# Gates and memory queries of layer one by seven half products; head norms, states and memory attention placed by slots; three row blocks begun with five rows of weights

## The chip, the cores and the metric

One core of one Trainium2 chip runs the kernel. The metric is device microseconds (us) of one launch, the median of several runs. Five engines work side by side: TensorE (PE: matmuls, all in float32 here, and transposes), VectorE (DVE), ScalarE (ACT), GpSimd (POOL) and SyncE (SP), which here only issues DMAs. They are ordered by semaphores alone, which the program sets by hand.

## The reference

One step of a decoder of two layers, on 1024 prompt rows and 8 sample rows (W = 1032 columns once they are laid side by side), model width 1024. The change touches layer one, cut here to what matters:

```python
h = _rmsnorm(x, g_pre);  z = h @ w_in_a                      # 1024 -> 4096
u, o_pre, zg, qm, zm = split(z, [1024, 2048, 3072, 3584])
# u gives q, k, v; a scan over 8 chunks of 128 gives hs for 4 heads of 256
C_new = dc * C + einsum('s,sv,sk->vk', ws, v, k)              # also for 8 x 4 sample states
h = sigmoid(o_pre) * hs
hn = (h - mean(h)) * rsqrt(var(h) + EPS) * g_hn               # per head
ya = (hn + skip * xc) * silu(zg)
ym = mem_attention(qm, mk, mv) * silu(zm)                     # 256 memory rows, 4 heads of 128
x = x + _rmsnorm(concat([ya, ym]) @ w_out_a, g_post)
```

Layer two (windowed attention and memory attention) then follows in the same manner. The 32 sample states C (8 samples, 4 heads, 256x256) are read, decayed, updated and written back.

## The kernel before

Activations lie transposed: HT holds h as eight tiles of 128 features by 1032 columns, BIG holds 24 such tiles, a head h of layer one having six of them from 6h on. RING is three slots of weights, PS eight PSUM banks. The stages, in the order in which TensorE meets them:

- Stages 0 and 1: memory keys and values, the norm, the projections u, q, k, v, the gate rows, and the first o projection pair (o0). They stay as they are.
- Stage 2 (`stage2_pe` and its like on each engine): 32 units, 8 chunks by 4 heads. In a unit TensorE makes scores (L744), transposes v and k (L750, L752), transposes the finished rows of two units ago (L762), then the numerator (L772, L775) and the state update (L783). L762 waits for `ct_done`, which DVE gives by its two updates of L866. On DVE a unit is L837 (q scaled, both inputs in SBUF), L841 (scores by decay), three tiny operations (L852 to L859), L866 twice. POOL only adds the mask to each chunk's rows (L728). Behind the loop the states of the prompt are transposed (L882).
- Stage 3 (`stage3_pe`, `stage3_act`, `stage3_dve`, `stage3_pool`, `stage3_sp`): the projections zg0, then o, zg of the heads 1 to 3, each by `pe_proj` (L301): 8 weight tiles times 3 segments of 344 columns, 24 matmuls. Between them come the averages of a head over its features (L1071, `average`), which wait for DVE's sums. DVE works in the order of the heads: for each, eight sample states (`pair_dve`: L1031 a reduce, L1036 two updates), the gate o as one operation of 2064 columns (L1204), the sum of both tiles (L1206), and between the next head's states the centring (L1170), the sum of squares (L1163), the norm (L1150, L1153) and the gate zg (L1158). ACT applies sigmoid and silu while it reads a projection out of PSUM (L1130, L1137), takes the squares (L1097), makes the root by Ln and Exp (L1105, L1107) and decays states (L1024). POOL multiplies a state by q (L1017). SP loads and stores states in three buffers of XTRA.
- Stage 4: the queries qmA and the gates zmA of the memory attention by the same kind of projection (L301, L1819), 4 tiles each. While zmA runs, the 18 steps of `step_pe` (scores L1670, transposes L1682, values L1702) are woven between its matmuls; their softmax lies on DVE (L1741 to L1759) and ACT (L1723). The silu of zmA comes when all of it is done (L1636).
- Stage 5 (`out_pe`): the output projection by blocks of 128 rows, each 12 weight rows `kt` (8 of the heads, 4 of the memory attention) by two halves of 512 columns (L1970); the last rows by columns (L2014). Block 0 and block 1 run their 8 head rows first, block 2 comes whole after both. The samples' attention is woven in (L1453, L1469, L1514).
- Layer two (`layer_b_*`): its projections go by pairs of output tiles, `PAIRS`. The half-size blocks of weights and activations are combined so that seven products do the work of eight (`ORDER`: A11 B11, S2 T2, A12 B21, S3 T3, S1 T1, A22 T4, S4 B22). A pair has two units (column halves, `BOUNDS` 0-256-512 and 512-772-1032), a unit seven products of four matmuls (L2844), a product is a **slot**, 14 slots a pair. POOL makes the weight sums (`sum_pair`, L2460 to L2464), DVE the four activation sums T (`h_sum`, L2401), once per layer. Of a unit's products ACT copies two out of PSUM (j = 0 and 2, L2929), DVE adds the other five (`product_sum_dve`, L3023 to L3034), and all else in layer two is placed by the number of the slot.

`product_waits` is what binds TensorE to these:

```python
elif j == 2: pe.wait_ge(*copied(u, 0))      # ACT's copy of product 0
elif j == 3: pe.wait_ge(*summed(u, U2))     # DVE's sum of product 1
elif j == 6: pe.wait_ge(*summed(u, C22))    # DVE's sum of product 4
```

So the sums of the products 1 and 4 must be done one slot after their product ended; those of 3, 5 and 6 have two slots or more.

## Time and profile before

| | us |
|---|---|
| median of 3 runs (lowest, highest) | 1902.46 (1899.45, 1902.49) |
| the profiled execution, its own time | 1904.15 |
| its span in the trace | 1902.4 |
| PE busy in the span | 1858.9 (98%) |
| DVE / ACT / POOL busy | 772.0 / 591.8 / 361.2 |
| PE's share of the chain that ended last | 89% |
| data moved | 196.14 MB |

The profile lists each float32 matmul as two records, so its counts are twice those of the code. The end of a matmul record is modelled and reaches past the start of the next: how fast TensorE streams is read from the length of an unbroken run of records, divided by their number, not from the mean duration of one. A group of instructions is named by the line of the kernel that issued it.

### The profile page before, as it was taken

The numbers are of one execution on the slowest core, as the hardware profiler recorded it, in microseconds if no ns is written. First come the engines' busy times: TensorE is split into PE (matmuls) and PEld (weight loads), VectorE is DVE, ScalarE is ACT, GpSimd is POOL, SyncE is SP. The second block draws the span as 40 slices with busy tenths as digits, with TensorE's granted clock in tenths as the row PEclk, the third lists the DMA queues.
The fourth block names the chain that finished last, engine by engine and source line by source line (L and its number), as shares of the span: only waits on it lengthen the run. The fifth ranks groups of instructions, "written<-read, shape, count | busy, mean of one in ns | idle before, by whom it ended". The sixth has DMA issues, their size and how long they took to land.

```text
span 1902.4 us, 21176 instructions
## 1 busy us (share of the span) xinstructions
PE 1858.9 (98%) x8117; PEld 1368.1 (72%) x8117; DVE 772.0 (41%) x1470; ACT 591.8 (31%) x1362; POOL 361.2 (19%) x309
## 2 busy tenths in 40 slices
PE   7999999999999999999999999999999999999998
PEld 3566664678666666765756888888888888878673
DVE  0332210555253542445144254335434544676523
ACT  1512231555243322341131122432233234643311
POOL 0000000010131110122002344225422643122100
PEclk9999999999999999999999999999999999999999
DMA  7311210211555652464110111123223342845322
GB/s 270 108 66 61 68 45 11 69 37 45 132 189 166 210 166 80 87 197 135 45 68 32 45 45 57 62 73 100 79 68 99 92 155 90 269 134 159 130 89 90
DMA packets 163215, 196.14 MB, mean 103 GB/s; under 512 B 19275, under 2 KB 122315, under 8 KB 162978
## 3 DMA queue, kind: packets, MB, share of 16 engines
q1 hardware_dynamic: 132628, 163.49, 27.6%
q10 hardware_dynamic: 30486, 31.30, 5.3%
q8 instruction: 65, 1.06, 0.2%
q14 instruction: 36, 0.29, 0.1%
HBM read 156.97 MB, written 37.85 MB: 102 GB/s over the span
## 4 chain that ended last, share of the span: by engine, by line
PE 89%; DVE 3%; ACT 3%; issue 2%; DMA 1%; POOL 1%; SPq 0%; ACTq 0%; DVEq 0%; POOLq 0%
PE PS L2844 29%; PE PS L301 17%; PE PS L1970 10%; PE PS L502 4%; PE PS L2014 4%; PE PS L1670 3%; PE PS L1819 3%; PE PS L381 3%; PE PS L512 2%; PE PS L1705 2%; PE PS L1682 2%; PE PS L1702 1%; PE PS L783 1%; PE PS L775 1%; DVE WK L866 1%
## 5 line engine op out<-in xcount | busy, mean ns | idle before, releaser
L301 PE MATMUL PS<-HT,RING 128*128 128x344 f32 x1344 | 391.2, 453 | 1.6 <-DVE HT L459 1.2
L301 PEld LDWEIGHTS PS<-HT,RING 128*128 128x128 f32 x1344 | 254.9, 190 | 135.9 <-DVE HT L459 2.0
L2844 PE MATMUL PS<-HT,RING 128*128 128x260 f32 (+1 forms) x1152 | 293.3, 383 | 1.2 <-ACT BIG L2929 1.2
L2844 PEld LDWEIGHTS PS<-HT,RING 128*128 128x128 f32 x1152 | 213.1, 191 | 29.4 <-ACT BIG L2929 1.9
L1970 PE MATMUL PS<-BIG 128*128 128x512 f32 x352 | 156.9, 596 | 0.0
L1723 ACT ACTIVATE WK<-PS,WK 128x256 f32<-128x256 f32 (+1 forms) x160 | 68.9, 435 | 189.6 <-DVE WK L1741 186.3
L2929 ACT ACTIVATE BIG<-PS 128x256 f32<-128x256 f32 (+1 forms) x96 | 37.0, 386 | 258.5 <-PE PS L2844 258.4
L1970 PEld LDWEIGHTS PS<-BIG 128*128 128x128 f32 x352 | 64.9, 190 | 72.4 <-issue 72.2
L1741 DVE TENSOR_REDUCE WK<-PS 128x2 f32<-128x512 f32 (+1 forms) x80 | 48.3, 604 | 108.0 <-PE PS L1670 107.8
L728 POOL TENSOR_TENSOR WK<-WK,CST 128x512 f32<-128x512 f32 x8 | 10.2, 1281 | 424.4 <-DMA WK<-mlstm_rows 424.4
L2844 PE MATMUL PS<-HT,CST 128*128 128x256 f32 (+1 forms) x336 | 86.4, 382 | 0.1
L1017 POOL TENSOR_TENSOR WK<-XTRA 128x512 f32<-128x512 f32 x32 | 48.6, 1522 | 199.8 <-DMA XTRA<-sample_q_and_weighted_k 161.5
L502 PE MATMUL PS<-WK,RING 128*128 128x344 f32 x288 | 83.9, 452 | 0.0
L2438 ACT ACTIVATE RING<-RING,VEC 128x256 f32<-128x256 f32 x176 | 75.0, 502 | 1.7 <-DMA RING<-in_w_in_b 0.8
L502 PEld LDWEIGHTS PS<-WK,RING 128*128 128x128 f32 x288 | 54.7, 190 | 28.7
L2844 PE MATMUL PS<-WK,RING 128*128 128x256 f32 x288 | 73.8, 380 | 0.0
L2844 PE MATMUL PS<-BIG,RING 128*128 128x260 f32 x288 | 71.4, 384 | 0.2 <-DVE BIG L3023 0.2
L3043 DVE TENSOR_TENSOR BIG<-BIG,TRIG 64x1024 f32<-64x1024 f32 (+1 forms) x48 | 71.2, 1482 | 1.1
L2844 PEld LDWEIGHTS PS<-HT,CST 128*128 128x128 f32 x336 | 61.7, 190 | 8.6 <-DVE BIG L3028 0.8
L2713 POOL TENSOR_TENSOR BIG<-BIG 128x512 f32<-128x512 f32 x48 | 61.0, 1282 | 13.4 <-DVE BIG L3052 13.4
L381 PE MATMUL PS<-RING,BIG 128*128 128x512 f32 x128 | 59.0, 622 | 3.2 <-ACT BIG L413 2.0
L1819 PE MATMUL PS<-HT,RING 128*128 128x344 f32 x192 | 61.8, 453 | 0.0
(350 smaller groups left out, 2930.4 us busy)
## 6 DMA issues: line engine op xcount, KB each, us to landing
WK<-in_cache_mem_kv SPq DMA_DIRECT2D x56, 256.0 KB, 5.8
RING<-in_w_kv_b SPq DMA_DIRECT2D x12, 1024.0 KB, 5.3
RING<-in_w_in_b SPq DMA_DIRECT2D x12, 1024.0 KB, 5.3
RING<-in_w_in_a ACTq DMA_DIRECT2D x21, 512.0 KB, 4.2
WK<-in_cache_win SPq DMA_DIRECT2D x40, 256.0 KB, 5.0
RING<-in_w_mkv SPq DMA_DIRECT2D x16, 512.0 KB, 4.7
BIG<-in_x_prompt SPq DMA_DIRECT2D x16, 512.0 KB, 3.2
XTRA<-in_state_C SPq DMA_DIRECT2D x32, 256.0 KB, 3.4
```

The source lines that it names most:

```text
L301: last = nc.tensor.matmul(PS[:, s + b, 0:SEG], w[:, kt * P:(kt + 1) * P], rhs(kt, b * SEG, (b + 1) * SEG), start=(kt == 0), stop=(kt == kt ...
L381: last = nc.tensor.matmul(PS[:, 4 * l + 2 * nt + half, :], MEMT[:, kt, nt * P:(nt + 1) * P], w[:, half * 512:(half + 1) * 512], start=(kt ...
L502: last = nc.tensor.matmul(PS[:, s + b, 0:SEG], w[:, c:c + P], rhs, start=(kt == 0), stop=(kt == 1))
L1670: last = nc.tensor.matmul(bank[:, x * nk:(x + 1) * nk], q, k, start=(g in MEM), stop=True, skip_group_check=True)
L1723: last = nc.scalar.activation(PROB[:, u % 2, x * nk:(x + 1) * nk], PS[:, 3 + u % 2, x * nk:(x + 1) * nk], ACT.Exp, bias=negmax[:, x:x + 1] ...
L1819: last = nc.tensor.matmul(PS[:, b, 0:SEG], w[:, kt * P:(kt + 1) * P], ht(kt, b * SEG, (b + 1) * SEG), start=(kt == 0), stop=(kt == KT - 1))
L1970: last = nc.tensor.matmul(PS[:, BANKS[i] + half, :], c.src(kt, u * P, (u + 1) * P), c.piece(kt)[:, half * 512:(half + 1) * 512], start=(kt ...
L2014: last = nc.tensor.matmul(PS[:, 6 + n % 2, 0:COLS], c.piece(kt)[:, n * P:(n + 1) * P], c.src(kt, 6 * P, W), start=(kt == 0), stop=(kt == c ...
L2438: last = nc.scalar.activation(x, x, ACT.Copy, scale=VEC[:, k, row:row + 1])
L2713: last = nc.gpsimd.tensor_tensor(perm(dst, d)[:, j0:j1], natural(big(RAW + x, 0, T), d)[:, j0:j1], natural(big(TURN + x, 0, T), d)[:, j0:j ...
L2844: last = nc.tensor.matmul(PS[:, bank, 0:mid - lo], weight_block(u // 2, s, k), h_block(u % 2, t, k), start=(k == 0 and j not in (2, 3, 6)) ...
L3043: last = nc.vector.tensor_tensor(y[q:q + 64], x[p:p + 64], TRIG[p:p + 64, W + lo:W + hi] .rearrange("p (t n) -> p t n", t=1).to_broadcast( ...
```

## The change

In layer one, 22 projection tiles (zg0 to zg3, o1 to o3, the memory queries and their gates) now go by the seven products too, as 11 pairs in the order zg0, o1, zg1, o2, zg2, o3, qm01, qm23, zg3, zm01, zm23, with bounds 0-258-516 and 516-774-1032: 154 slots. Of TensorE's matmuls nothing else changes in kind or number: 528 of 344 columns become 616 of 258. The stages 3 and 4 become one table of slots, `layer_a_*`:

```diff
-        for h in range(H):
-            if h > 0:
-                oz_jobs(h, D, "o")
...
+        for x, first in (("Azg0", 2 * D), ("Ao1", D + 2 * P), ("Azg1", 2 * D + 2 * P), ("Ao2", D + 4 * P),
+                         ("Azg2", 2 * D + 4 * P), ("Ao3", D + 6 * P), ("Aqm01", 3 * D), ("Aqm23", 3 * D + 2 * P),
+                         ("Azg3", 2 * D + 6 * P), ("Azm01", 3 * D + 4 * P), ("Azm23", 3 * D + 6 * P)):
+            PAIRS.append((x, w_in_a, first, None))
+        PA = len(PAIRS)
...
+        EARLY_AT = (17, 18, 19, 23, 25, 27, 29, 31)
...
+        XA = 14 * PA
+        GATE, GATED_3 = (4, 31, 58, 86), 128
+        MEAN = [x + 3 for x in GATE]
+        VAR = [x + 9 for x in GATE]
+        KEYS_A, STEPS_A = 112, 116
...
+        def states_at(x):
+            return [i for i in range(EARLY_STATES, H * NS) if 3 + 7 * (i - EARLY_STATES) // 2 == x]
...
+        def layer_a_dve(dve):
+            for x in range(XA + 1):
+                if x >= 1:
+                    product_sum_dve(dve, x - 1)
+                for i in states_at(x - 1):
+                    pair_dve(dve, i)
+                for h in range(H):
+                    head_dve(dve, x, h)
+                for s in steps_a(x):
+                    step_dve(dve, MEM_A, s)
+                for n in keys_a_at(x - 1):
+                    samples_scores_dve(dve, "A", [n])
```

`head_dve` cuts a head's work into operations of one tile (1032 columns) at fixed slots behind `GATE[h]`: n = 0, 1 the gate o (n = 0 also the sample part), 2 the sum for the mean, 4, 5 the centring, 8 the sum of squares, 12, 13 and 14, 15 the norm, 16, 17 the gate zg (head 3: slots 128, 129). The averages stand inside the slots `MEAN` and `VAR` on TensorE and wait there for DVE. Sigmoid and silu are now applied by ACT in place, on two tiles of half the columns, one slot after a unit is complete (`gate_act`), so the silus of zg3 and zm fall among the steps of the memory attention, which begin at slot 116 and come every second slot.

Eight of the 32 sample states move into stage 2, behind the units of `EARLY_AT`, on POOL, ACT, DVE and SP; the other 24 come every three or four slots, with a fourth buffer. POOL, not DVE, makes layer one's sums of activations:

```diff
+            if c == 2:
+                pool.wait_ge(job_done.sem, done("o0_1"))
+                for gi in range(2):
+                    h_sum(pool, "A", gi, T1)
+                sum_pair(pool, 0)
...
+            pool.wait_ge(sig("kv_turned").sem, NU - 2)
+            h_sum(pool, "A", 0, T2), h_sum(pool, "A", 0, T3)
+            pair_pool(pool, EARLY_STATES - 1)
```

In stage 5 five weight rows come first, in each of the blocks 0, 1 and 2, and then the other seven of each; the samples' values move behind with them:

```diff
-                self.kts, self.early, self.src, self.piece = kts, kts - H, src, piece
+                self.kts, self.early, self.src, self.piece = kts, 5 if kts > KT else 4, src, piece
...
-            block_products(pe, x, 0, early[:4])
+            block_products(pe, x, 0, early)
             free1(pe)
             samples_pe(pe, x)
-            block_products(pe, x, 0, early[4:])
...
+            block_products(pe, x, 1, early)
+            samples_turned_pe(pe, x)
+            if x == "A":
+                block_products(pe, x, 2, early)
```

The weight rows 2 and 3 are loaded once the last unit but one is done, the rows 5 to 7 once the last product is.

On TensorE, from the end of stage 2 on, before (L301 a projection of 24, L1071 an average):

```order
L783 MATMUL PS<-WK 128x257 x2
L882 MATMUL PS<-CST,WK 128x128 x8
L762 MATMUL PS<-CST,WK 128x128 x2
L882 MATMUL PS<-CST,WK 128x128 x8
L301 MATMUL PS<-HT,RING 128x344 x96
L1071 MATMUL PS<-BIG,CST 128x344 x3
```

and now (L2952 is a product's matmul, L896 the old L882, L1198 the old L1071):

```order
L793 MATMUL PS<-WK 128x257 x2
L896 MATMUL PS<-CST,WK 128x128 x8
L772 MATMUL PS<-CST,WK 128x128 x2
L2952 MATMUL PS<-HT,RING 128x258 x4
L2952 MATMUL PS<-BIG,WK 128x258
L896 MATMUL PS<-CST,WK 128x128 x8
L2952 MATMUL PS<-BIG,WK 128x258 x3
L2952 MATMUL PS<-HT,RING 128x258 x4
L2952 MATMUL PS<-BIG,RING 128x258 x4
L2952 MATMUL PS<-HT,RING 128x258 x4
L2952 MATMUL PS<-BIG,RING 128x258 x4
L2952 MATMUL PS<-HT,CST 128x258 x4
```

The average that had four whole projections ahead of it now has seven products and one matmul.

On DVE, the gate of head 1 (behind 16 states) with the states around it, before:

```order
L1031 TENSOR_REDUCE SM<-WK 128x2
L1036 SCALAR_TENSOR_TENSOR XTRA<-XTRA,SM 128x256 x2
L1196 TENSOR_TENSOR SM<-SM 128x16
L1197 TENSOR_TENSOR SM<-SM 128x16
L1199 TENSOR_TENSOR BIG<-SM 128x2x8
L1204 TENSOR_TENSOR BIG<-BIG 128x2064
L1206 TENSOR_TENSOR BIG<-BIG 128x1032
L1031 TENSOR_REDUCE SM<-WK 128x2
```

and now (L1070 and L1075 are a state, L1335 the gate o of one tile, L1338 the sum, L31xx sums of products):

```order
L1317 TENSOR_TENSOR SM<-SM 128x16
L1318 TENSOR_TENSOR SM<-SM 128x16
L1320 TENSOR_TENSOR BIG<-SM 128x2x8
L1335 TENSOR_TENSOR BIG<-BIG 128x1032
L3137 TENSOR_TENSOR BIG<-BIG,PS 128x258
L1070 TENSOR_REDUCE SM<-WK 128x2
L1075 SCALAR_TENSOR_TENSOR XTRA<-XTRA,SM 128x256 x2
L1335 TENSOR_TENSOR BIG<-BIG 128x1032
L3140 TENSOR_TENSOR BIG<-BIG,PS 128x258
L1338 TENSOR_TENSOR BIG<-BIG 128x1032
L3143 TENSOR_TENSOR BIG<-BIG,PS 128x258
L3146 TENSOR_TENSOR BIG<-BIG,PS 128x258
```

The sums that TensorE waits for within a slot now stand in DVE's queue behind whole-tile operations and states.

## Rows read from the trace of the kernel before

**Rows 1.** The page's first part: busy time, share of the span, instructions.

```profile
PE 1858.9 (98%) x8117; PEld 1368.1 (72%) x8117; DVE 772.0 (41%) x1470; ACT 591.8 (31%) x1362; POOL 361.2 (19%) x309
```

**Rows 2.** Stretches (us: length, PE PEld DVE ACT POOL busy, PEclk, DMA, GB/s).

```profile
360.80:480.80 120.00, 111.63 (x648) 94.47 (x649) 66.48 (x243) 67.04 (x167) 11.05 (x9) 1.00 0.15 42
480.80:840.50 359.70, 356.18 (x1373) 243.21 (x1371) 154.13 (x242) 111.13 (x179) 66.71 (x47) 1.00 0.52 147
840.50:1024.00 183.50, 183.50 (x638) 106.96 (x637) 64.87 (x104) 39.28 (x91) 13.97 (x9) 1.00 0.28 98
1042.80:1132.20 89.40, 89.40 (x412) 78.09 (x413) 31.46 (x49) 16.81 (x43) 30.98 (x30) 1.00 0.15 47
```

**Rows 3.** The chain that ended last, in order of time: start, length, what.

```profile
556.00 41.64 PE PS L301 x144
...
840.64 6.87 PE PS L1970 x16
...
1281.86 38.25 PE PS L2844 x176
```

**Rows 4.** Groups of TensorE between 480.8 and 840.4 us.

```profile
L301 PE MATMUL PS<-HT,RING 128*128 128x344 f32 x864 | 251.3, 452 | 0.0
L1819 PE MATMUL PS<-HT,RING 128*128 128x344 f32 x192 | 61.8, 453 | 0.0
```

**Rows 5.** Waits of TensorE between 480 and 841 us: total, times, longest.

```profile
PE PS L1071 <- DVE BIG L1163: 1.8, 1, 1.8
```

**Rows 6.** DVE in stage 2, in order of time, and POOL's operation there.

```profile
425.21 1.45 DVE L837 TENSOR_TENSOR WK<-BIG,WK 128x256 f32<-128x256 f32 x1
...
430.18 0.29 DVE L841 TENSOR_TENSOR WK<-PS,WK 128x128 f32<-128x128 f32 x1 [0.97 <-ACT WK L811]
430.71 0.16 DVE L852 SCALAR_TENSOR_TENSOR SM<-PS,SM 128x1 f32<-128x1 f32 x1 [0.24 <-PE PS L775]
...
431.57 0.88 DVE L866 SCALAR_TENSOR_TENSOR WK<-WK,PS 128x257 f32<-128x257 f32 x2 [0.32 <-PE PS L783]
...
425.11 1.27 POOL L728 TENSOR_TENSOR WK<-WK,CST 128x512 f32<-128x512 f32 x1 [12.32 <-DMA WK<-mlstm_rows]
```

**Rows 7.** By source line: shortest, median, longest (ns), first and last start.

```profile
L837 DVE TENSOR_TENSOR WK<-BIG,WK x32: 415/418/1497, 359.1 to 471.7; 128x256 f32<-128x256 f32 x32
L1031 DVE TENSOR_REDUCE SM<-WK x32: 674/682/690, 480.4 to 691.2; 128x2 f32<-128x512 f32 x32
L1036 DVE SCALAR_TENSOR_TENSOR XTRA<-XTRA,SM x64: 469/479/1484, 487.3 to 692.2; 128x256 f32<-128x256 f32 x64
L1163 DVE TENSOR_TENSOR BIG<-BIG x4: 1233/1434/2053, 552.6 to 707.9; 128x1032 f32<-128x1032 f32 x4
L3023 DVE TENSOR_TENSOR BIG<-BIG,PS x48: 410/422/427, 1028.8 to 1755.0; 128x256 f32<-128x256 f32 x24, 128x260 f32<-128x260 f32 x24
L1105 ACT ACT_TABLE_LOAD  x4: 1283/1283/1283, 555.0 to 718.4; - x4
L1137 ACT ACTIVATE BIG<-PS x8: 1010/1031/1034, 494.9 to 687.9; 128x1032 f32<-128x1032 f32 x8
```

**Rows 8.** Groups by engine and shape (busy us, mean ns, idle before).

```profile
L1036 DVE SCALAR_TENSOR_TENSOR XTRA<-XTRA,SM 128x256 f32<-128x256 f32 x64 | 30.8, 523 | 60.8 <-ACT XTRA L1024 60.3
L1163 DVE TENSOR_TENSOR BIG<-BIG 128x1032 f32<-128x1032 f32 x4 | 6.2, 1538 | 8.0 <-ACT BIG L1097 8.0
L2462 POOL TENSOR_TENSOR WK<-RING 128x512 f32<-128x512 f32 x12 | 19.2, 1603 | 0.9
L1017 POOL TENSOR_TENSOR WK<-XTRA 128x512 f32<-128x512 f32 x32 | 48.6, 1522 | 199.8 <-DMA XTRA<-sample_q_and_weighted_k 161.5 <-PE PS L783 35.9 <-DVE SM L1031 2.3
```

**Rows 9.** DMA issues: KB each, median us from issue to landing.

```profile
RING<-in_w_in_b SPq DMA_DIRECT2D x12, 1024.0 KB, 5.3
XTRA<-in_w_out_a ACTq DMA_DIRECT2D x3, 512.0 KB, 8.8
```

More of the change, by code:

```diff
@@ new lines, in gate_applied, with tiles2, keys_a_at, steps_a @@
+        def gate_applied(kind, n):
+            u = 2 * [x[0] for x in PAIRS].index(kind) + n
+            return sig("tables_applied").sem, sum(1 for k in range(u + 1) if gated(k))
+        TABLES_A = sum(1 for k in range(2 * PA) if gated(k))
+        def tiles2(t, lo=0, hi=W):
+            return BIG[:, :].rearrange("p (i w) -> p i w", w=W)[:, t[0]:t[1] + 1:t[1] - t[0], lo:hi]
+        def keys_a_at(x):
+            return [n for n in range(2 * NS) if 122 + 2 * n == x]
+        def steps_a(x):
+            return [s for s in range(18) if STEPS_A + 2 * s == x]
@@ new lines, in layer_a_pool @@
+        def layer_a_pool(pool):
+            for x in range(XA):
+                for i in states_at(x + 1):
+                    pair_pool(pool, i)
+                if x == 6:
+                    pool.wait_ge(sig("h_turned").sem, NU)
+                    sum_pair(pool, 1)
+                p = x // 14 + 1
+                if x % 14 == 9 and 2 <= p < PA:
+                    sum_pair(pool, p)
+                samples_pool(pool, "A", keys_a_at(x))
+            samples_pool(pool, "A", [n for n in range(2 * NS) if 122 + 2 * n >= XA])
@@ L1066, in average @@
+        AVERAGED = PS[:, 3:6, 0:SEG]
         def average(pe, name, h, summed):
-            pe.wait_ge(*slot_free(name))
             pe.wait_ge(sig(summed).sem, h + 1)
+            if name == "mean0":
+                pe.wait_ge(sig("c_copied").sem, H)
+            else:
+                pe.wait_ge(*read_of(f"mean{h}" if name[0] == "v" else f"var{h - 1}"))
             for b in range(3):
-                last = nc.tensor.matmul(PS[:, slot_of(name) + b, 0:SEG], avg_h,
-                                        big(h * 6 + 2, b * SEG, (b + 1) * SEG), start=True, stop=True)
+                last = nc.tensor.matmul(AVERAGED[:, b, :], avg_h, big(HELD[h][0], b * SEG, (b + 1) * SEG),
+                                        start=True, stop=True)
@@ new lines, in woven_a_pe, with layer_a_pe, first_copy_act @@
+            if x == KEYS_A + 2:
+                memory_query_pe(pe, 0)
+                yield
+            for s in steps_a(x):
+                yield from step_pe(pe, MEM_A, s)
+        def layer_a_pe(pe):
+            for x in range(XA):
+                woven = woven_a_pe(pe, x)
+                product_pe(pe, x, woven)
+                for _ in woven:
+                    pass
+        def first_copy_act(act, u):
+            kind = PAIRS[u // 2][0]
+            if kind == "Ao2":
+                act.wait_ge(sig("conv_saved").sem, 32 + 16 * H)
+            if kind == "Azg2":
+                act.wait_ge(sig("y_ready").sem, 2)
+            if kind == "Ao3":
+                act.wait_ge(sig("squares_summed").sem, 2)
+                act.wait_ge(job_done.sem, done("var0"))
+            if kind == "Aqm01":
+                act.wait_ge(job_done.sem, done("var1"))
+            if kind == "Aqm23":
+                act.wait_ge(sig("y_ready").sem, 4)
+                act.wait_ge(job_done.sem, done("var2"))
+            if kind == "Azg3":
+                act.wait_ge(sig("y_ready").sem, 6)
+            if kind == "Azm01":
+                act.wait_ge(job_done.sem, done("var3"))
+            if kind == "Azm23":
+                act.wait_ge(sig("squares_summed").sem, 3)
@@ L2077, in both @@
                 hold(kt)
-            block_products(pe, x, 2, range(c.kts), both)
-            column_products(pe, x, 0, early)
+            block_products(pe, x, 2, range(c.kts) if x == "B" else late, both)
+            column_products(pe, x, 0, own)
             pe.wait_ge(sig("sample_out_read").sem, order + 1)
-            column_products(pe, x, 0, late)
+            column_products(pe, x, 0, cross)
             for n in range(1, KT):
```

767 lines of the change are left out of this document (385 added, 382 removed).

## The prediction

> **What bounds the kernel now.** I read the page's busy times first: TensorE (PE) is busy for 1858.9 of 1902.4 us, DVE for 772.0 [rows 1]. Busy time can hide small gaps, because the ends of matmuls are modelled, so I took two more views. The stretches show where PE has room: from the end of stage 2 to the start of the output projection it lacks 3.5 us of 359.7, in the output projection nothing of 183.5, in stage 2 8.4 of 120.0 [rows 2]. The chain of waits gives the pace of an unbroken run: 144 records of 344 columns in 41.64 us, 0.2892 us each, and 176 records of layer two's products, 256 and 260 columns in equal parts, in 38.25 us, 0.2173 us each [rows 3]. Both are near 0.84 ns per column. The kernel streams columns from end to end, at the full clock (granted 1.00 in these stretches [rows 2], the 2.4 GHz level). So a column less is worth 0.84 ns twice over, and nothing else brings anything unless it removes one of the few waits. A change that gives other engines more to do costs time only where PE comes to wait.
>
> **Columns.** Between 480.8 and 840.4 us lie 864 + 192 = 1056 records of 344 columns [rows 4]: 22 tiles of 24 matmuls, two records each. At 0.2892 us they take 305.4 us. The 154 products have 616 matmuls, 1232 records of 258 columns, the mean width of the run in layer two: 1232 x 0.2173 = 267.7 us. **-37.7 us**. The weights of a matmul change every 258 columns now and not every 344; the same run in layer two shows no cost of that, its 0.2173 us holds it. All other matmuls keep their number and width in the order of the instructions, so that the change does what it says on PE can be taken as settled.
>
> **Waits that go.** The 3.5 us of idle PE in that stretch [rows 2] are mostly one average waiting 1.8 us for DVE [rows 5], and the places where the others lie are laid out anew. **-3 us**; I price the new ones apart.
>
> **Stage 2.** 32 units fill 120 us, some 3.6 us each [rows 2]. DVE is idle in it for 0.97 + 0.24 + 0.32 = 1.53 us, and its L866 stands on PE's path: PE goes on with L762 when it is done [rows 6]. A state adds 0.68 + 2 x 0.48 = 1.64 us to DVE [rows 7], 0.1 us more than that room, and some 0.1 us for its semaphores; ACT's decay and POOL's product have room or lie on another engine. Eight states, the last of them behind the last unit: 1.5 us. Then POOL. In rows 6 DVE's L837, two operands from SBUF, takes 1.45 us and not 0.42, beside a POOL operation of 1.27 us that began 0.10 us earlier; the longest L837 took 1.50 [rows 7], while L3023, one of whose operands is PSUM, never passes 0.43 [rows 7]. Its delay of 1.03 us disappeared in the 1.53. The activation sums on POOL have 1032 columns: 1.27 x 1032 / 512 = 2.6 us if it goes by length, so they can delay L837 by up to 2.5 us, 1.0 beyond the room. Of the eight, two fall at the start and three before the last unit: 4.5 us with the states' updates caught too. **+6 us**, ends 1.5 (no operation is caught) and 12 (each early state is also caught once by 0.75 us). The early activation sums and the first weight sums themselves are hidden: the first product with a sum that comes late, S3 T3, begins 3.5 us after stage 2, and POOL's row of T2, T3, a state and T4 begins two units, 7 us, before its end. Without that cover a late sum would cost 2.6 us each.
>
> **DVE in the slots.** A slot is 8 x 0.2173 = 1.74 us. DVE's sum of a product takes 0.42 [rows 7]; products 1 and 4 of a unit leave it one slot. A head's whole-tile operations take 1.23 us at the least [rows 7]. At two places per head the queue is too full.
> - Gate and mean. Three slots and one matmul, 3 x 1.74 + 0.43 = 5.65 us, are there before PE wants the head's sum for its average. DVE has in them three tiles (3.7), a state (1.64), the sample part (0.5) and three product sums (1.26) for head 0: 7.1 us, 1.45 late; two product sums for the heads 1 and 2: 6.7, 1.05 late each; head 3 has no state there and is in time. 3.5 us.
> - Norm and gate zg. Six slots, 10.4 us, and about one slot of grace, for six tiles (7.6), two states (3.3) and four product sums (1.7), 12.6 us: 0.5 us for each of the heads 0 to 2, 1.5 us.
>
> That is 5 us with no operation lengthened. Operations with two operands in SBUF were lengthened on average from 0.48 to 0.52 (states) and from 1.23 to 1.54 (the sum of squares) [rows 7, 8], with POOL busy for 66.7 of 359.7 us [rows 2]. Now POOL has besides 24 states of 1.5 us [rows 8] ten weight sums of four operations near 1.5 and a short one, close to 7 us a pair of 24.3 us: half of the time up to slot 92. I take 0.15 us per operation, between 0.04 and 0.31: 15 of them in the first places, 2.3 us, and 30 in the second, of which half falls into the grace, 2.2 us. **+9.5 us**, ends 5 and 15 (0.3 us each).
>
> The page "SBUF — State Buffer" of the Trainium skill, in "Who interferes with whom", says that a DVE instruction with two SBUF inputs and a GpSimd instruction that reads SBUF exclude each other for the whole instruction, whoever comes first. By that rule alone, with POOL busy half of the time and half an operation left on average, the hold would be near 0.3 us, this term 15 and the whole sum 5.5 us higher. The trace agrees in kind: 1.45 against 0.42 [rows 6].
>
> **ACT beside the memory attention.** Silu among the Exps of the steps costs ACT two table loads of 1.28 and 1.03 us of work [rows 7], 3.6 us in a step of 2 x 1.74 us and 2.2 us of attention matmuls; between a step's scores and its transposes lie some 6 us of PE work against a chain of 3.3 us on DVE and ACT. It happens at slots 120, 127, 134, 141. **+1 us**, ends 0 and 6.
>
> **Output projection.** The same products, in another order, and PE had no gap in it [rows 2], so there is nothing to gain. Five rows of three blocks are 30 matmuls of 2 x 0.43 us [rows 3], 25.8 us before anything else is needed, against 27.5 before (two blocks of eight rows). The rows 2 and 3 are issued seven slots (12.2 us) before block 0, and 1 MB lands in 5.3 us, with ACT's rows beside it in up to 8.8 [rows 9]. **0**, ends 0 and 3.
>
> **Sum.** -37.7 - 3 + 6 + 9.5 + 1 = -24.2 us, on the profiled execution's 1904.15 us (its span is 1902.4) 1880.0. The profiled execution lies 1.7 above the median of the runs shown; for a median, 1902.46 - 24.2 = **1878 us**. With all low ends it is -34, with all high ends -5.
>
> **Rivals.**
> - Nobody waits. In layer two PE ran 89.4 us without a gap with DVE 35% and POOL 35% busy [rows 2]. If the queue's lateness is taken up by the slack of two slots, only 1.5 us of stage 2 remain: -39, 1863 us. Against it: layer one's DVE has 129 us of work in the first 92 slots (160 us), 80%.
> - DVE becomes the bound, and the kernel slower. Mechanism: POOL's operations hold DVE's two-operand ones. There are 48 state updates and 40 head operations up to slot 92. At 0.8 us each, near the longest holds seen (1.48 - 0.48, 2.05 - 1.23 [rows 7]), DVE's 129 us become 199 against 160: +39; stage 2 at 12, less 40.7: +10, 1913 us. It decides from about 0.7 us per operation. Against it: the mean holds of 0.04 and 0.31. The page named above makes it possible but does not give the holds.
> - States are late. The 32 states went from 487.3 to 692.2 us, 6.5 us each [rows 7], and POOL waited 161.5 us for their loads [rows 8]. Now one is due every 3.5 slots, 6.1 us, with a weight pair of 1 MB every 24.3 us in the same queue. If they come no faster, DVE stands still with product sums behind it: 24 x 0.5 = 12 us more, 1890 us. Against it: a fourth buffer, loads issued some 9 slots ahead, and DMA at 0.52 [rows 2], with ACT's pace, not the loads, behind half of the waits before.
>
> **How the numbers follow.** Forecast 66% (its own range 1868 to 1889), nobody waits 14%, states late 10%, DVE the bound 6%, other mishaps that end near or above the old time 4%. 0.2% is 3.8 us, about what a measurement of this kernel tells from no change. Faster by more: 91%; within: 2%; slower: 7%. The range for 8 in 10 is 1862 to 1893: it takes in the case without waits and late states, and leaves the bound DVE and the tail of the high ends out.
>
> **What would show it.** Right: no record of 344 columns but u, o0, qkv, gates and averages, runs of products at 0.217 us each, some 318 us from the last L793 to the first block plus 10 of waits; PE's waits led by products and averages (L1198) waiting for DVE near slots 6, 7, 20, 34, 40, 61 and 76; stage 2 longer by 4 to 8 us, with DVE's scaling of q at 2 us beside POOL's sums; output projection of 183 us as before. Wrong: PE idle by less than 5 us in the slots (first rival), POOL or DVE waiting for state loads (third), DVE busy above 90% up to slot 92 with updates near 1.3 us (second), or a gap at the first block, waiting for weights.

## The result and the profile after

In 15 runs each, the changed kernel took 1908.08 us in the median (1897.25 to 1916.08) and the kernel before 1900.7 us (1898.35 to 1903.93). The ratio is 1.0035, 95% interval 1.0023 to 1.0047: slower by 0.35%, where 1.3% faster was forecast, and outside the range. The profiled run took 1906.62 us, its span is 1904.8. The runs of the change spread over 19 us, those of the kernel before over 5.6; their mean granted clock lies between 0.987 (the run of 1916.08 us) and 0.995 (the run of 1897.25).

The busy times of the page answer to [rows 1]:

```profile
PE 1834.1 (96%) x8293; PEld 1405.8 (74%) x8293; DVE 838.9 (44%) x1588; ACT 606.1 (32%) x1397; POOL 446.8 (23%) x372
```

PE has 24.8 us less to do and the span is 2.4 us longer. The stretches answer to [rows 2], with the same columns (start:end, length, busy of PE, PEld, DVE, ACT, POOL, granted clock, DMA share, GB/s): stage 2, the slots of layer one, the output projection.

```profile
358.10:488.80 130.70, 114.63 (x640) 96.66 (x641) 87.39 (x264) 69.74 (x170) 43.04 (x29) 0.96 0.26 80
488.80:843.00 354.20, 331.50 (x1556) 280.73 (x1554) 198.54 (x342) 126.69 (x212) 122.09 (x93) 0.98 0.45 135
843.00:1026.50 183.50, 183.50 (x636) 107.04 (x637) 68.54 (x101) 35.54 (x87) 13.01 (x7) 1.00 0.26 95
```

From stage 2's first transposes to the first product it is now 130.8 us and was 119.7; from there to the output projection 354.2 and was 359.7. The output projection is unchanged, as forecast. Stage 2 began 3.1 us earlier, in code that the change doesn't touch: in the loading phase the trace of the kernel before has three stretches of 3.4 us at the half clock, that of the change one. So 2.4 = -3.1 + 11.1 - 5.5 - 0.1. The forecast had +6 for stage 2 and -30.2 for the slots. The other new thing is the granted clock: 0.96 and 0.98 where it was 1.00 twice. The waits of TensorE from 358 to 843 us, total, times and longest:

```profile
PE PS L772 <- DVE WK L878: 9.2, 3, 5.0
PE PS L2952 <- DVE BIG L3140: 6.4, 4, 2.2
PE PS L1198 <- DVE BIG L1338: 5.1, 3, 3.0
PE PS L2952 <- ACT BIG L3040: 4.7, 1, 4.7
PE PS L1198 <- DVE BIG L1348: 3.3, 3, 1.9
PE PS L2952 <- DVE BIG L3135: 2.5, 3, 1.0
```

L2952 is a product, L1198 an average, L772 a unit's turned values in stage 2. Three causes can be read from the trace.

**Stage 2's end.** DVE, then POOL, in order of time:

```profile
463.38 4.69 DVE L1075 SCALAR_TENSOR_TENSOR XTRA<-XTRA,SM 128x256 f32<-128x256 f32 x2
467.99 0.41 DVE L849 TENSOR_TENSOR WK<-BIG,WK 128x256 f32<-128x256 f32 x1
...
475.44 3.35 DVE L1075 SCALAR_TENSOR_TENSOR XTRA<-XTRA,SM 128x256 f32<-128x256 f32 x2
478.72 2.41 DVE L849 TENSOR_TENSOR WK<-BIG,WK 128x256 f32<-128x256 f32 x1
```

```profile
463.07 2.39 POOL L2502 TENSOR_TENSOR BIG<-HT 128x1032 f32<-128x1032 f32 x1
465.53 2.25 POOL L2502 TENSOR_TENSOR BIG<-BIG,HT 128x1032 f32<-128x1032 f32 x1
...
473.80 2.21 POOL L2502 TENSOR_TENSOR BIG<-BIG,HT 128x1032 f32<-128x1032 f32 x1
475.96 2.55 POOL L2502 TENSOR_TENSOR BIG<-HT 128x1032 f32<-128x1032 f32 x1
478.66 4.54 POOL L2502 TENSOR_TENSOR BIG<-BIG,HT 128x1032 f32<-128x1032 f32 x2
```

At 463 us both updates of a state (L1075) are held, each until the activation sum then running ends: together they take 4.69 us instead of 0.88. At 475 us the second update is held in the same way (3.35 us for the two), and q's scaling (L849) meets the next sum and takes 2.41 us. The sums come back to back, so an operation of DVE with two operands in SBUF that has stood out one of them can meet the next, and the delays add up: PE waits 3.5 us from 466.4 and 5.0 us from 477.6. With both waits TensorE's clock falls.

**Slot 14.** ACT, in order of time, POOL's product of a state, and the products of PE on both sides:

```profile
524.16 0.72 ACT L1061 ACTIVATE TRIG<-TRIG,SM 128x512 f32<-128x512 f32 x1 [6.98 <-POOL WK L1052]
524.90 1.28 ACT L1262 ACT_TABLE_LOAD   x1
526.19 1.12 ACT L1262 ACTIVATE WK<-PS,SM 128x1032 f32<-128x1032 f32 x1
527.33 1.28 ACT L1264 ACT_TABLE_LOAD   x1
528.63 1.06 ACT L1264 ACTIVATE WK<-WK 128x1032 f32<-128x1032 f32 x1
529.60 0.37 ACT L3040 ACTIVATE BIG<-PS 128x258 f32<-128x258 f32 x1
```

```profile
522.86 1.27 POOL L1052 TENSOR_TENSOR WK<-TRIG 128x512 f32<-128x512 f32 x1 [8.25 <-DMA TRIG<-sample_q_and_weighted_k]
```

```profile
523.38 1.91 PE L2952 MATMUL PS<-BIG,WK 128*128 128x258 f32 x8
530.02 3.81 PE L2952 MATMUL PS<-HT,RING 128*128 128x258 f32 x8 [4.73 <-ACT BIG L3040]
```

The copy of product 14 (L3040) stands behind head 0's root (Ln and Exp, each with a table load, 4.7 us), the root behind the decay of a state, and the decay waits 6.98 us for POOL's product, which waits 8.25 us for its load. The load was late in SP's queue, behind this wait for the small stores of stage 2's states and four loads of xc:

```profile
SPq L1138 <- DMA out_m_p<-SM: 12.9, 1, 12.9
```

**The clock.** Eight records (four matmuls) of 258 columns took 1.91 us before that wait and 3.81 us behind it. Six stretches at the level of 1.2 GHz lie in stage 2 and the slots, beginning at 470.8, 481.0, 528.8, 542.5, 627.8 and 661.9 us, and none in the kernel before. Three of them, with the columns as above, and the sum of the six:

```profile
470.80:474.20 3.40, 3.40 (x10) 2.74 (x9) 0.91 (x5) 1.18 (x3) 1.63 (x2) 0.50 0.24 85
...
528.80:535.60 6.80, 5.58 (x13) 4.45 (x14) 2.83 (x3) 5.12 (x7) 1.30 (x1) 0.50 0.70 238
542.50:545.90 3.40, 3.40 (x10) 2.65 (x9) 3.40 (x3) 0.00 (x0) 3.24 (x3) 0.50 0.18 45
...
sum 27.40, PE 24.46 PEld 18.96 DVE 11.66 ACT 8.24 POOL 16.23; mean PE 4.08 PEld 3.16 DVE 1.94 ACT 1.37 POOL 2.70
```

Each lies in or right behind a pause of PE of 2 us or more. In them PE is busy for 24.5 us, half of which is loss: some 12 us.

### The profile page after: what moved, and what is told of

It is laid out like the page before. It is cut to its first block, busy times and chain, and to the rows that moved or that the text cites. A ratio compares the mean times of both kernels' runs of the same rounds, so it can differ in the third digit from the quotient of the medians.

```text
span 1904.8 us, 21851 instructions
## 1 busy us (share of the span) xinstructions
PE 1834.1 (96%) x8293; PEld 1405.8 (74%) x8293; DVE 838.9 (44%) x1588; ACT 606.1 (32%) x1397; POOL 446.8 (23%) x372
## 4 chain that ended last, share of the span: by engine, by line
PE 87%; DVE 5%; ACT 3%; issue 3%; DMA 1%; POOL 1%; ACTq 0%; DVEq 0%; SPq 0%; POOLq 0%
PE PS L2952 40%; PE PS L2055 10%; PE PS L282 7%; PE PS L483 4%; PE PS L2099 4%; PE PS L1856 3%; PE PS L362 2%; PE PS L493 2%; PE PS L1891 2%; PE PS L1868 2%; PE PS L1888 1%; PE PS L793 1%; PE PS L785 1%; DVE WK L878 1%; PE PS L1694 1%
## 5 line engine op out<-in xcount | busy, mean ns | idle before, releaser
L2952 PE MATMUL PS<-HT,RING 128*128 128x260 f32 (+2 forms) x1680 | 425.1, 384 | 5.9 <-ACT BIG L3040 5.9
L2952 PEld LDWEIGHTS PS<-HT,RING 128*128 128x128 f32 x1680 | 313.6, 192 | 49.6 <-ACT BIG L3040 7.0
L3040 ACT ACTIVATE BIG<-PS 128x256 f32<-128x256 f32 (+2 forms) x140 | 54.0, 385 | 405.9 <-PE PS L2952 405.5
L282 PE MATMUL PS<-HT,RING 128*128 128x344 f32 x480 | 139.9, 453 | 1.6 <-DVE HT L440 1.2
L2952 PE MATMUL PS<-BIG,RING 128*128 128x260 f32 (+1 forms) x560 | 138.7, 383 | 1.1 <-DVE BIG L3135 1.0
L282 PEld LDWEIGHTS PS<-HT,RING 128*128 128x128 f32 x480 | 90.9, 190 | 50.3 <-DVE HT L440 2.0
L2952 PEld LDWEIGHTS PS<-BIG,RING 128*128 128x128 f32 x560 | 105.1, 191 | 17.5 <-DVE BIG L3135 1.9
L2952 PE MATMUL PS<-BIG,WK 128*128 128x258 f32 (+1 forms) x448 | 112.7, 385 | 1.5 <-DVE BIG L3135 1.5
L2952 PE MATMUL PS<-HT,CST 128*128 128x256 f32 (+2 forms) x432 | 110.8, 383 | 1.3 <-DVE BIG L3140 1.2
L2952 PEld LDWEIGHTS PS<-BIG,WK 128*128 128x128 f32 x448 | 84.4, 193 | 14.4 <-DVE BIG L3135 2.5
L2952 PEld LDWEIGHTS PS<-HT,CST 128*128 128x128 f32 x432 | 79.4, 190 | 13.6 <-DVE BIG L3140 3.2
L2952 PE MATMUL PS<-WK,RING 128*128 128x256 f32 x288 | 73.8, 380 | 0.0
L3137 DVE TENSOR_TENSOR BIG<-BIG,PS 128x256 f32<-128x256 f32 (+1 forms) x70 | 29.5, 422 | 97.7 <-PE PS L2952 97.4
```

The source lines that it names most:

```text
L282: last = nc.tensor.matmul(PS[:, s + b, 0:SEG], w[:, kt * P:(kt + 1) * P], rhs(kt, b * SEG, (b + 1) * SEG), start=(kt == 0), stop=(kt == kt ...
L2952: last = nc.tensor.matmul(PS[:, bank, 0:mid - lo], weight_block(u // 2, s, k), h_block(layer_of(u), u % 2, t, k), start=(k == 0 and j not ...
L3040: nc.scalar.activation(big(n2 if j == 0 else n1, lo, mid), PS[:, banks(u)[0], 0:mid - lo], ACT.Copy).then_inc(sig("projections_copied").up ...
```

## The experiments

All are edits of the changed kernel. Each was timed in five rounds against the kernel before on its chip (the probe and the last one in three). "Against the change" is the ratio's difference from 1.0035, times 1901 us; two such ratios have together an uncertainty of 3 to 4 us, near 5 for the probe and the last run. The last two columns are from each trace: from stage 2's first transposes to the first product, and from there to the output projection (the kernel before: 119.7 and 359.7).

| run | ratio to before (95%) | against the change | stage 2 | slots |
|---|---|---|---|---|
| the change | 1.0035 (1.0023 to 1.0047) | | 130.8 | 354.2 |
| e1, late activation sums narrow | 0.9972 (0.9960 to 0.9984) | -12.0 | 119.4 | 352.0 |
| e2, root behind the copy | 1.0012 (0.9996 to 1.0029) | -4.4 | 132.3 | 350.0 |
| e3, POOL's slot work narrow | 0.9960 (0.9949 to 0.9972) | -14.3 | 132.2 | 339.0 |
| e4, slot states narrow | 0.9948 (0.9936 to 0.9960) | -16.5 | 131.7 | 336.3 |
| e5, xc's loads at slot 10 | 0.9996 (0.9982 to 1.0009) | -7.4 | 131.6 | 342.9 |
| e6, sums shared with DVE | 0.9971 (0.9958 to 0.9985) | -12.2 | 119.7 | 351.8 |
| e7, e5 and e6 | 0.9952 (0.9938 to 0.9966) | -15.8 | 119.7 | 345.5 |
| e8, six pauses in layer two | 1.0118 (1.0099 to 1.0136) | +15.8 | 132.7 | 352.5 |
| e9, e7 and a state first | 0.9950 (0.9936 to 0.9965) | -16.2 | 119.6 | 344.6 |
| e10, e9 and averages later | 0.9943 (0.9930 to 0.9956) | -17.5 | 119.4 | 346.4 |
| e11, averages later alone | 1.0000 (0.9989 to 1.0011) | -6.7 | 132.8 | 345.9 |
| e12, all light | 0.9847 (0.9825 to 0.9868) | -35.7 | 119.9 | 330.5 |

### e1: the late activation sums narrow

```diff
+            if layer == "A" and (gi, t) != (0, T1) and (gi, t) != (1, T1):
+                out, x, y = out[:, :, 0:8], x[:, :, 0:8], y[:, :, 0:8]
             on.tensor_tensor(out, x, y, ALU.subtract).then_inc(sig("h_sums").up(), 1)
```

> The changed kernel with the six activation sums that GpSimd makes at the end of stage 2 cut from 258 columns a block to 8, so that part of the activations' sums is left out; all waits stay. Theory of the holds: the long gaps at 466.1 (3.64 us) and 477.2 (5.18 us) come from DVE's updates of two SBUF operands being held for some 2 us each by these sums of 2.3 to 2.6 us, and the 10 us at the half clock behind them follow from the gaps: stage 2 falls from 130.7 to 120 to 123 us and the kernel by 8 to 11 us. Theory of the full queue: the eight states' updates alone fill DVE in stage 2: the kernel falls by 3 us at the most and stage 2 stays above 127.

Measured: -12.0 us, stage 2 at 119.4 with a granted clock of 1.00. The whole 11 us of stage 2 come from six operations on an engine off the critical path. That is the theory of the holds; the full queue's would have left stage 2 above 127 us. The eight early states cost nothing: with them stage 2 is as long as before.

### e2: head 0's root behind the copy

```diff
-                    if x == VAR[h] + 1:
+                    if x == VAR[h] + (2 if h == 0 else 1):
                         root(act, h)
```

> The changed kernel with ACT's logarithm and exponential of head 0's variance one slot later, behind the copy of product 14 and no longer ahead of it. If that order makes the gap of 4.89 us at 524.9 and, through it, the 6.8 us at the half clock behind it (3.4 us lost), the kernel falls by 5 to 8 us. Rival: the norms on DVE and all behind them are then late instead, and the gap only moves to a product that waits for DVE: less than 2 us.

Measured: -4.4 us, between the two expectations. The wait for the copy fell from 4.7 to 0.3 us, but the root, now at 529.3 to 534.0 us, made the norms late, and a product sum behind them: one wait of 5.5 us, for L3140 at slot 20. The order of root and copy is a link of the chain, not its start.

### e3: POOL's work in the slots narrow

The ten weight sums (from the second pair on) and the 24 state products of the slots are cut to 8 columns; DVE reads another tile of the same width for the state's sum.

```diff
-                QWP(i, 0, 256).unsqueeze(1).to_broadcast([P, 2, 256]), ALU.mult)
+                QWP(i, 0, m).unsqueeze(1).to_broadcast([P, 2, m]), ALU.mult)
...
+            if 1 <= p < PA:
+                cut = lambda t: t[:, :, 0:8]
+                a11, a21, a22, s2, s3 = cut(a11), cut(a21), cut(a22), cut(s2), cut(s3)
```

> The changed kernel with GpSimd's part of the slots of layer one taken down to 8 columns an operation (the ten weight sums from the second pair on and the 24 state products, so that these parts of the computation are left out); DVE and ACT keep all their instructions and widths. Theory of the holds: DVE's operations of 2 us there return to 0.42 and 1.23 us, PE's idle 23 us in the slots falls below 12, and fewer half-clock stretches follow: the kernel falls by 12 to 18 us. Theory of the full queue: DVE has too much at the places of the heads whatever GpSimd does: 6 us at the most, and the waits for the sums of the heads stay.

Measured: -14.3 us, the slots 15.2 us shorter, with DVE's instructions and widths all there. The groups of DVE between 488 and 843 us show why: busy time and mean ns of one, first in the change, then here (each line number is one higher):

```profile
L1075 DVE SCALAR_TENSOR_TENSOR XTRA<-XTRA,SM 128x256 f32<-128x256 f32 x38 | 27.4, 763 | 0.7 <-ACT XTRA L1061 0.7
L1368 DVE TENSOR_TENSOR BIG<-BIG 128x1032 f32<-128x1032 f32 x8 | 13.8, 1726 | 0.6 <-ACT BIG L1269 0.6
L1360 DVE SCALAR_TENSOR_TENSOR BIG<-WK,VEC,BIG 128x1032 f32<-128x1032 f32 x8 | 12.9, 1629 | 0.1
L1343 DVE TENSOR_TENSOR BIG<-BIG,PS 128x1032 f32<-128x1032 f32 x8 | 9.7, 1219 | 0.0
L1338 DVE TENSOR_TENSOR BIG<-BIG 128x1032 f32<-128x1032 f32 x4 | 8.1, 2026 | 0.0
```

```profile
L1076 DVE SCALAR_TENSOR_TENSOR XTRA<-XTRA,SM 128x256 f32<-128x256 f32 x38 | 16.6, 479 | 0.6 <-ACT XTRA L1062 0.5
L1361 DVE SCALAR_TENSOR_TENSOR BIG<-WK,VEC,BIG 128x1032 f32<-128x1032 f32 x8 | 10.1, 1286 | 0.1
L1369 DVE TENSOR_TENSOR BIG<-BIG 128x1032 f32<-128x1032 f32 x8 | 10.0, 1245 | 0.6 <-ACT BIG L1270 0.6
L1344 DVE TENSOR_TENSOR BIG<-BIG,PS 128x1032 f32<-128x1032 f32 x8 | 9.7, 1221 | 0.0
L1339 DVE TENSOR_TENSOR BIG<-BIG 128x1032 f32<-128x1032 f32 x4 | 4.9, 1232 | 0.0
```

The updates, the skip's addition (L1360), the gate zg (L1368) and the head's sum (L1338), with two operands in SBUF, are held; the centring (L1343), one of whose operands is PSUM, takes 1219 and 1221 ns. The head's sum lost 0.8 us in the mean of the four heads, and its average is what PE waits for next.

The Trainium skill, "SBUF — State Buffer", section "Who interferes with whom", says that a DVE instruction with two SBUF inputs contends with a GpSimd instruction that reads SBUF, and one with at most one SBUF input does not. The traces agree on both sides: L1360 takes 1629 ns beside GpSimd's full work and 1286 beside the narrow one, L1343 1219 and 1221, though in the change GpSimd was busy as four of its eight began. The trace of the change also shows why only some are held: the other whole-tile operations with two SBUF operands (L1335, L1348, L1353) kept their 1.2 to 1.3 us, and none of them began while GpSimd was busy.

### e4: the states of the slots narrow

```diff
-                c = CTP(i, vt * 256, (vt + 1) * 256)
+                c = CTP(i, vt * 256, vt * 256 + m)
```

with m = 8 for the 24 states of the slots, in DVE's sum and POOL's product too; the weight sums stay whole.

> The changed kernel with the 24 states of the slots cut to 8 columns in GpSimd's product, DVE's sum and DVE's update (left out of the computation); loads, stores and ACT's decay stay, and so do the weight sums. It takes 1.64 us of DVE and 1.3 us of GpSimd away every 3.5 slots. Theory of the full queue: nearly all waits of the heads go: 15 to 20 us. Theory of the holds: the weight sums still hold the heads' operations, half of the gain of the run without GpSimd's work: 6 to 10 us. If the late state loads are what matters, less than 4 us, since the loads stay as late as they are.

Measured: -16.5 us, in the range that the theory of the full queue gave, as e3's gain was in that of the holds; each edit also touches the other's cause, since the 48 updates narrowed here are among the operations that GpSimd holds. Taking away POOL's part (e3) or the states' part of both engines (this run) gives nearly the same, 15.2 and 17.9 us of the slots, and it does not add up: with both of them and e5's edit (e12) the slots lose 23.7 us. That the delays arise where a full queue and a hold meet fits all three; no run separates the two. Both runs kept a single wait of 4.2 to 5.2 us for ACT's copy at slot 14, which e5 explains.

### e5: xc's loads later in SP's queue

```diff
-                if x == 4:
+                if x == 10:
                     sp.wait_ge(sig("c_copied").sem, H)
                     sp.wait_ge(sig("states_saved").sem, STATES)
                     load_xc(sp, 0), load_xc(sp, 1)
```

> The changed kernel with SP's piece of slot 4 (its wait for the small stores of the stage-2 states, 12.9 us in the trace of the change, and the four loads of xc behind it) issued at slot 10, so that the loads of the states of slots 10 and 13 don't stand behind it; nothing else moves. Theory of the late state: the product on GpSimd for slot 10 came at 522.9 us because its load stood in SP's queue behind that wait; ACT's decay waited for it ahead of head 0's root, the root ahead of the copy of product 14, and PE 4.9 us for that copy. Then the gap falls below 1.5 us, one half-clock stretch goes with it, and the kernel falls by 5 to 8 us. Rival: the root alone (4.7 us with its table loads) fills the time between the average and the copy whatever the state does: less than 2 us.

Measured: -7.4 us, the slots 11.3 us shorter. PE's waits there hold none for ACT any more, and the clock is at 1.00 over the slots instead of 0.98:

```profile
494.10:837.00 342.90, 325.79 (x1555) 276.41 (x1553) 198.60 (x342) 126.74 (x211) 120.59 (x93) 1.00 0.47 139
```

So the start of that chain is a wait in SP's queue which nobody on the critical path asked for. Only one stretch of 3.4 us at the half clock was left in the slots of this trace, where the change's had four, 17 us in all. With stage 2 at 0.8 us more the two stretches are together 10.5 us shorter. The time fell by 7.4, within the uncertainty of the two ratios; the two profiled runs differ by 4.1 only, mostly since stage 2 begins 4.4 us later in this one (362.5 against 358.1 us).

### e6 and e7: the activation sums shared by two engines

```diff
+                    if u == NU - 1:
+                        dve.wait_ge(sig("kv_turned").sem, NU)
+                        h_sum(dve, "A", 0, T2)
...
+            h_sum(dve, "A", 0, T3), h_sum(dve, "A", 0, T4)
```

DVE makes the first group's three, GpSimd the second group's behind them. The second kernel has e5's edit besides.

> The changed kernel with three of the six late activation sums on DVE behind stage 2's last update of the states, and the other three on GpSimd after those, in slots 2 to 6; nothing is left out. Theory of the holds: stage 2 falls from 129 to 118 to 121 us as in the run with narrow sums, the first products wait for T2 by up to 1 us, and the kernel falls by 7 to 11 us. Rival: DVE's 3.5 us more at the start of the slots make head 0 later by as much, and it gives back all but 3 us.

> Both edits of the two runs before together (xc's loads at slot 10, the activation sums shared by DVE and GpSimd). If the two causes are separate the gains add: 12 to 18 us below the change, 1890 to 1896 us, below the kernel before as well (ratio 0.993 to 0.997). If head 0 is simply too full, the second edit takes back the first one's gain: 8 us at the most.

Measured: -12.2 and -15.8 us, nothing left out. Stage 2 is at 119.7 in both. e7 is faster than both kernels, 0.9952 of the one before, but less than the sum of the parts (19.6). In e7's trace DVE shows a new wait at the start of the slots:

```profile
489.61 0.42 DVE L3137 TENSOR_TENSOR BIG<-BIG,PS 128x258 f32<-128x258 f32 x1 [3.06 <-PE PS L2952]
494.18 0.69 DVE L1070 TENSOR_REDUCE SM<-WK 128x2 f32<-128x512 f32 x1 [4.14 <-POOL WK L1052]
...
496.24 2.18 DVE L1335 TENSOR_TENSOR BIG<-BIG,TRIG 128x1032 f32<-128x1032 f32 x1
498.34 0.41 DVE L3140 TENSOR_TENSOR BIG<-BIG,PS 128x258 f32<-128x258 f32 x1
```

The state of slot 3 waits for a product that GpSimd makes behind the three sums, and the product sum (L3140) for which PE waits 5.7 us at slot 6 stands behind that state.

### e8: pauses where there were none

```diff
+        PROBE = {10: 400, 24: 900, 38: 1400, 52: 1900, 66: 2900, 80: 4400}
...
+            if x - XA in PROBE:
+                pe.wait_ge(sig("probe").sem, list(PROBE).index(x - XA) + 1)
```

DVE raises `probe` after a reduction of so many columns, begun when the product before is done.

> The changed kernel with six pauses of PE set into layer two's first 84 slots, which had none: before the products of slots 10, 24, 38, 52, 66 and 80 PE waits for a DVE reduction of 400, 900, 1400, 1900, 2900 and 4400 columns, begun when the product before it is done; nothing is left out. The pauses should be near 0.7, 1.2, 1.7, 2.2, 3.3 and 4.8 us, 14 us in all. If a pause costs only its length, layer two grows by 13 to 15 us with the granted clock at 1.00. If the longer ones also bring the clock down, as the gaps of 2 us and more in layer one did, there is a half-clock stretch behind the last two or three, each worth 1.7 to 3.4 us more, and layer two grows by 18 to 24.

Measured: stretches around the pauses, with the columns as above (the second and the third, not shown, lack 1.27 and 1.79 us at 1.00):

```profile
1044.00:1054.00 10.00, 9.25 (x43) 7.73 (x42) 4.30 (x6) 0.78 (x2) 7.40 (x6) 1.00 0.01 2
...
1120.00:1132.00 12.00, 9.68 (x45) 8.10 (x45) 7.69 (x7) 0.78 (x2) 7.36 (x6) 1.00 0.00 0
1150.00:1164.00 14.00, 10.31 (x42) 8.44 (x41) 8.30 (x7) 1.37 (x3) 8.11 (x6) 0.88 0.00 0
1182.00:1200.00 18.00, 12.83 (x54) 10.80 (x53) 10.31 (x8) 1.94 (x5) 7.33 (x5) 0.81 0.08 29
```

Length less PE's busy time gives the pauses: 0.75, 1.27, 1.79, 2.32, 3.69 and 5.17 us, 15.0 in all. Behind the first four the clock stayed; with the last two it fell. A mean of 0.88 over 14 us is some 3.4 us at the half clock, 0.81 over 18 us some 6.8, of which PE ran about 4, since this fall began within the pause. From the output projection on, the trace is 18.4 us longer (1080.2 against 1061.8): 15.0 of pauses and 3.7 of slow running. The median grew by 15.8. So a pause of 3.7 us costs near 5.4, and one of 5.2 costs 7.

Whether a pause of some 2 us brings the clock down is not a fixed thing. The longest wait of an average for the sum of the squares (head 1's) is 1.9 us in the traces of the change and of e1 alike; there was no fall behind it in the change, and a stretch of 3.4 us at the half clock in e1. In the change 2.0 us of waiting from 540.0 were enough, here 2.3 were not. The other traces widen that: 3.0 us at the average of head 2 brought the clock down in the change and not in e1, e5 and e6, and 3.4 us in the slots of e10 did not either, while all pauses of 4 us and more had a fall in or behind them. That fits the spread of the change's runs, 19 us, with the mean clocks from 0.987 to 0.995; what decides it in the single case was not tried.

### e9, e10 and e11: two more repairs

e9 is e7 with this edit:

```diff
-            h_sum(pool, "A", 1, T2), h_sum(pool, "A", 1, T3), h_sum(pool, "A", 1, T4)
+            h_sum(pool, "A", 1, T2)
...
+                if x == 2:
+                    h_sum(pool, "A", 1, T3), h_sum(pool, "A", 1, T4)
```

e10 has this besides, and e11 has this alone:

```diff
-        MEAN = [x + 3 for x in GATE]
-        VAR = [x + 9 for x in GATE]
+        MEAN = [x + 4 for x in GATE]
+        VAR = [x + 10 for x in GATE]
...
+            n -= 1
             if n in (4, 5):
```

> The kernel of the run with both edits, with GpSimd's product for the state of slot 3 ahead of the last two activation sums of the second group and no longer behind them. There DVE waited 6.3 us for that product, from 487.9 to 494.2, and then three of its operations stood in front of a product sum for which PE waited 5.9 us, at the half clock afterwards. If the wait of DVE is the cause, the gap at slot 5 falls below 3 us and the kernel by 3 to 6 us more, to 1885 to 1889. Rival: the sums then hold DVE's gate operations of head 0 for 2 us each instead, and the gap stays above 4 us: less than 1.5 us.

> The kernel of the run before with each head's average of the values and all that follows it (centring, squares, second average, root, norms, gate) one slot later, so that DVE has four slots and not three between the gates and the average. If the waits of the averages for DVE (5.5 us in four places there) come from the three slots being too short, they fall below 2 us, and the kernel by 3 to 5 us more, to 1881 to 1886. Rival: DVE's queue is late as a whole, and the waits move to the product sums: no change within 1 us.

> The change itself with only that shift of the averages by one slot; it also puts head 0's root behind the copy of product 14. By the theory of too few slots at the heads' places, the waits of the averages (8.4 us in six places) fall below 3 us: the kernel falls by 5 to 9 us together with the half-clock stretches behind the longer ones. If GpSimd's holds and SP's wait are what counts, PE waits as long for product sums instead: 3 us at the most.

Measured: e9 gained 0.4 us on e7 and e10 another 1.3, both within the intervals; e11 gained 6.7 on the change. In e9 the wait at slot 6 (slot 5 in the expectation) fell from 5.7 to 3.5 us only: GpSimd's two sums now hold that state's update, 2.41 us for its second half. So the sums held DVE as the rival said, but a state's update and not the gate operations (1.23 us each); the gain is of the rival's size, the wait between the two. In e11 the waits of the averages fell as expected, from 8.4 to 2.3 us, but those for the first sums of a unit rose from 2.5 to 7.8:

```profile
PE PS L2953 <- DVE BIG L3136: 7.8, 6, 3.4
...
PE PS L1198 <- DVE BIG L1349: 2.3, 2, 1.9
```

So three slots were too short for the first place of a head, but a fourth slot mostly moves the lateness to the product sums. The kernel's gain of 6.7 us is no proof of the first theory: the edit also puts head 0's root behind the copy, which by itself was worth 4.4 (e2).

### e12: everything light

The edits of e1, e3, e4 and e5 together.

> The change with everything light that was made light by itself before: the six late activation sums, the ten weight sums from the second pair on, the 24 states' product, sum and update in the slots all cut to 8 columns (left out of the computation), and xc's loads at slot 10. All products, averages and head operations on DVE stay. If the columns term of the prediction (-37.7 us against the kernel before) is right and only waits took it back, stage 2 takes 118 us, the slots 325 to 330, and the kernel 1864 to 1870 us. Rival: part of the columns' gain is lost in the products themselves (weights that change every 258 columns); then the slots stay above 335 with few waits in the profile.

Measured: 1871.5 us, 35.7 below the change, 29 below the kernel before; the expectation was missed by little, the kernel by 1.5 us, the slots by 0.5 and stage 2 by 2. Stage 2 and the slots:

```profile
361.20:481.30 120.10, 110.75 (x641) 93.79 (x642) 78.75 (x265) 69.65 (x170) 30.58 (x29) 1.00 0.29 87
481.30:811.40 330.10, 323.03 (x1553) 276.99 (x1552) 151.72 (x341) 126.45 (x211) 50.86 (x93) 0.99 0.51 145
```

The longest wait left is 2.3 us. The columns' gain is real and whole. The rival of a loss in the products themselves is out: in its slots 1160 of the 1172 steps from one product's record to the next are 0.2178 us in the mean, against the 0.2173 that the prediction took.

## Why the prediction was wrong, point by point

- **Columns, -37.7.** Right. Priced by their columns at the full clock, the records of the slots add up to 318.4 us where they added up to 355.0: 36.6 us less, and e12 shows the time without most waits.
- **Output projection, 0.** Right: 183.5 us again. The early rows of weights were not tried by themselves.
- **ACT beside the memory attention, +1.** Right in kind and nearly in size: two waits of 1.0 us each, at 753 and 794 us. At the first, DVE's product sum stands behind a step that waited 3.1 us for ACT's Exp, and ACT had a silu and two table loads of 1.28 us ahead of it.
- **Stage 2, +6, ends 1.5 and 12.** The mechanism was right and named, the size off by five: 11.1. The step that failed is the count of holds. The prediction let a sum delay DVE by 1.0 us beyond the room, once per sum, 4.5 us in all. The trace shows sums back to back that hold both halves of a state's update in one unit, and one half and then q's scaling in another, so that two units lose 3.5 and 5.0 us. And the prediction priced idle time at its own length, with nothing for the clock; the clock at 0.5 for 10.3 us behind those waits (8.7 us of them busy) added some 4. The early states, which it gave 1.5, cost nothing (e1).
- **DVE in the slots, +9.5, ends 5 and 15.** This is where the forecast broke: the slots exceed that sum of 318.4 us by 35.8 (idle time and slow records), against 4.7 before, where the prediction comes to 4.7 - 3 + 9.5 + 1 = 12.2. Its first part held: without holds (e3) PE waits for DVE in the slots 7.8 us, of which 2.0 are the attention's, against the 5 worked out. Four things were missing or too small:
  - The holds. Over the 90 operations of DVE with two operands in SBUF they come to 22.7 us (the groups shown and 12 updates at 653 ns), 0.25 us each, where 0.15 was taken and 0.31 was the upper end. But they don't lie evenly: the head's sum, the last one before an average, had 0.8. PE's waits for DVE are 17.3 us, 9.5 more than in e3, where the prediction had 4.5.
  - The copy of slot 14, 4.7 us. The section on waits looked at ACT only beside the memory attention, and not at where the root stands against a copy.
  - SP's queue. The rival of late states was the nearest to it, but it blamed the pace of the transfers; what made one load late, and with it that copy, was a wait of 12.9 us for other stores ahead of it (e5). What SP waits for at slot 4 was not followed.
  - The clock, which the prediction put at nothing. 17.1 us of the slots at the half clock, some 8 us lost.
- **Rivals.** "Nobody waits" (1863) is near what e12 shows with the work taken away (1871.5). "DVE becomes the bound" had the right mechanism and the right sign; a mean hold of 0.25 us was enough and not 0.7, since it was worked out as total work against total time, and the waits come from single deadlines missed.

The terms add up: between the forecast of -24.2 us and the +2.4 us of the trace lie 26.6 us, 23.6 of waits and slow clock in the slots, 5.1 of stage 2 and 1.1 of columns, less the 3.1 of the earlier start and 0.1.

What is open: how the extra time divides between waiting and slow clock in the median run. The profiled run is one draw from runs that spread by 19 us. And e3 and e4 took away work, so that they bound the causes (15 and 18 us of the slots) and don't add up. How much of the lateness is DVE's full queue and how much GpSimd's holds stays open too.

## What to carry to other kernels

Where an engine off the critical path gets work, look at its longest back-to-back run, not its mean share: each DVE operation with two operands in SBUF that falls into the run can be held by up to a whole instruction of it, one after the other, and the room must hold them all. Price a long wait of PE higher than its length (here 3.7 us cost 5.4), and count on one of 2 to 3 us costing more in some runs. And follow each in-order queue that issues loads (SP here) past every wait in it: one piece moved there was worth 7 us, and with the sums shared between two engines besides the change is worth 0.5% instead of costing 0.35%.

## What was not expected of the hardware

- In a kernel whose version before stayed at the full clock from 62 to 1669 us, six pauses of 2.0 to 5.0 us came with stretches of 3.4 and 6.8 us at the 1.2 GHz level. Pauses up to 2.3 us in the probe did not, nor did some of 3.0 and 3.4 us in e1, e5, e6 and e10.
- The changed kernel's runs spread by 19 us where the kernel before spread by 5.6, and the mean clock goes with the time. A kernel with many pauses near 2 us has to be timed in more runs.
- The holds go both ways. GpSimd's operations of a weight sum take longer too where DVE's whole-tile ones run beside them. Here, in the trace of the change, DVE's L1360, held until the first of the two ended at 540.54, ran on until 541.63, and the second took 2.25 us instead of 1.45:

```profile
539.09 1.45 POOL L2567 TENSOR_TENSOR RING<-RING 128x512 f32<-128x512 f32 x1
540.50 2.25 POOL L2568 TENSOR_TENSOR RING<-RING 128x512 f32<-128x512 f32 x1
```
